# Depthwise-convolution taps on TensorE: full-array diagonal matmuls, or 16 tiles of 32x32 with four taps at a time

## The reference, cut to what matters

```python
D_MODEL, SEQ, CONV_WIDTH = 1024, 512, 31

def causal_dwconv(x, w, b):             # x: (B, S, C), w: (31, C)
    y = lax.conv_general_dilated(x, w[:, None, :], window_strides=(1,), padding=[(30, 0)],
        dimension_numbers=("NWC", "WIO", "NWC"), feature_group_count=c)
    return y + b

def conformer_conv_module(h, w_in, b_in, dw, dw_b, ln_g, ln_b, w_out, b_out):
    u = h @ w_in + b_in                                  # 1024 -> 2048
    u = u[..., :D_MODEL] * jax.nn.sigmoid(u[..., D_MODEL:])
    u = causal_dwconv(u, dw, dw_b)                       # 31 taps, each channel alone
    u = layer_norm(u, ln_g, ln_b)
    u = jax.nn.silu(u)
    return u @ w_out + b_out
```

## Time and profile before

| | us |
|---|---|
| median of 3 runs | 3459.36 (3456.99 to 3459.85) |
| the profiled execution, device time | 3458.37 |
| its span, first to last instruction | 3456.6 |
| PE busy | 3280.9 (95%) |
| DVE busy | 1811.6 (52%) |
| ACT busy | 1227.3 (36%) |
| POOL busy | 138.6 (4%) |

### The profile page before, as it was taken

How to read it: one execution, slowest core, us unless ns; L and a number is a source line. 1 busy time by engine, 2 the same in 40 slices (tenths; PEclk the granted TensorE clock), 3 DMA queues, 4 the chain that set the end, 5 groups by cost and what they waited for, 6 DMA issues and landing times.

```text
span 3456.6 us, 41804 instructions
## 1 busy us (share of the span) xinstructions
PE 3280.9 (95%) x16765; PEld 2676.6 (77%) x16765; DVE 1811.6 (52%) x2360; ACT 1227.3 (36%) x1664; POOL 138.6 (4%) x148
## 2 busy tenths in 40 slices
PE   7889999999998899999999988999999999999999
PEld 6666888888876478888888647888788888888887
DVE  3756445554446744455536965554434524456543
ACT  2525224343334432344424324443312212244432
POOL 1121000000021300000000010000000000000000
PEclk9999999999999899999999989999999999999999
DMA  5220322222341122222232112222221221223222
GB/s 153 54 71 25 98 97 97 87 96 97 98 105 47 37 63 96 97 98 97 91 104 74 49 55 86 97 91 91 92 93 61 74 74 62 86 68 105 94 92 85
DMA packets 231695, 288.16 MB, mean 83 GB/s; under 512 B 5396, under 2 KB 188716, under 8 KB 231564
## 3 DMA queue, kind: packets, MB, share of 16 engines
q1 hardware_dynamic: 225628, 266.89, 23.7%
q0 software_dynamic: 5936, 19.40, 2.6%
HBM read 284.18 MB, written 2.10 MB: 83 GB/s over the span
## 4 chain that ended last, share of the span: by engine, by line
PE 88%; DVE 7%; ACT 3%; issue 2%; DMA 0%; DVEq 0%; POOL 0%; ACTq 0%; POOLq 0%
PE ps L1398 18%; PE ps L1399 18%; PE ps L1400 18%; PE ps L1495 6%; PE ps L1496 6%; PE ps L1497 6%; PE ps L1431 2%; PE ps L1433 2%; PE ps L1432 2%; PE ps L1564 2%; PE ps L1600 2%; PE ps L1744 1%; ACT t_whi L577 1%; DVE t_wlo L905 1%; PE ps L1838 1%
## 5 line engine op out<-in xcount | busy, mean ns | idle before, releaser
L905 DVE TENSOR_TENSOR t_wlo<-t_wraw,t_whi 128x2048 fp32r<-128x2048 f32 x252 | 578.7, 2296 | 1324.6 <-ACT t_whi L577 1324.6
L1398 PE MATMUL ps<-t_hh,t_whi 128*128 128x512 f32 (+1 forms) x2624 | 985.4, 376 | 45.4 <-DVE t_hl L975 27.1
L577 ACT ACTIVATE t_whi<-t_wraw 128x2048 fp32r<-128x2048 f32 x252 | 482.7, 1916 | 1472.7 <-PE ps L1400 981.8
L1399 PE MATMUL ps<-t_hl,t_whi 128*128 128x512 f32 (+1 forms) x2624 | 977.8, 373 | 0.0
L1400 PE MATMUL ps<-t_hh,t_wlo 128*128 128x512 f32 (+1 forms) x2624 | 977.6, 373 | 0.0
L1398 PEld LDWEIGHTS ps<-t_hh,t_whi 128*128 128x128 f32 x2624 | 502.8, 192 | 136.9 <-issue 22.5
L1399 PEld LDWEIGHTS ps<-t_hl,t_whi 128*128 128x128 f32 x2624 | 502.6, 192 | 85.1 <-issue 2.0
L1400 PEld LDWEIGHTS ps<-t_hh,t_wlo 128*128 128x128 f32 x2624 | 502.4, 191 | 83.9
L1497 PE MATMUL ps<-t_whi,t_midl 128*128 128x512 f32 x704 | 273.9, 389 | 0.0
L1495 PE MATMUL ps<-t_whi,t_midh 128*128 128x512 f32 x704 | 273.9, 389 | 0.0
L1496 PE MATMUL ps<-t_wlo,t_midh 128*128 128x512 f32 x704 | 273.9, 389 | 0.0
(11 more groups left out here) (246 smaller groups left out, 3968.0 us busy)
## 6 DMA issues: line engine op xcount, KB each, us to landing
t_wraw<-in_w_in_dram SPq DMA_DIRECT2D x46, 1024.0 KB, 5.3
t_wraw<-in_w_up_dram SPq DMA_DIRECT2D x44, 1024.0 KB, 5.1
t_wraw<-in_ffn_w_in_dram SPq DMA_DIRECT2D x44, 1024.0 KB, 5.0
t_wraw<-in_w_kv_dram SPq DMA_DIRECT2D x24, 1024.0 KB, 5.2
t_wraw<-in_w_down_dram SPq DMA_DIRECT2D x20, 1024.0 KB, 5.0
t_wraw<-in_ffn_w_out_dram SPq DMA_DIRECT2D x20, 1024.0 KB, 5.0
t_wraw<-in_w_branch_dram SPq DMA_DIRECT2D x12, 1024.0 KB, 5.0
t_wraw<-in_w_q_dram SPq DMA_DIRECT2D x12, 1024.0 KB, 5.1
```

What stands on the lines that cost most here:

```text
L577: sc.activation(whi[slot][:, :], wraw[slot][:, :], ACT.Copy).then_inc(w_hi, 1)
L905: v.tensor_tensor(wlo[slot][:, :], wraw[slot][:, :], whi[slot][:, :].bitcast(F32), ALU.subtract).then_inc(w_lo, 1)
L1398: te.matmul(out, wh, xh, start=first, stop=False)
L1399: te.matmul(out, wh, xl, start=False, stop=False)
```

## The change

The taps on TensorE no longer use the whole array for one tap. A weight is now a diagonal of 32x32 for 32 channels, and the array is used as 16 tiles: four groups of 32 channels (rows of the array, index i) times four taps (columns, index g). `partial_taps(t)` (L1799 of the changed kernel) issues, for each four taps of a channel tile, 16 matmuls of 32x32 by 512; tap g of channel group i goes to PSUM bank `part_bank(t, i)`, partitions 32g to 32g + 31. So each channel has four partial sums, on four groups of partitions. ACT copies the four banks to SBUF (`copy_partials`, L889), and `join_taps(t)` (L1807) adds the four partial sums with one matmul for each channel group, whose weight is four 32x32 identities stacked (`stack`, a new constant). DVE adds the result to `vb` (`add_joined`, L1327).

With it other things change. PE takes 16 taps of each of the first six tiles and 20 of the last two (`pe_taps`), where it took 10; DVE takes 15, 15, 15 and 11 in the four steps (DVE_TAPS), where it took 21. The diagonals are made by POOL, one instruction for a channel tile (`tap_diagonals`, L565), from `stack`, which POOL loads first. The mean of the layer norm takes two matmuls: POOL adds up the tiles 0 to 6 (`usum`, L578 and L581) as they become complete, and PE multiplies `usum` and the last tile.

The order on PE is another: the taps of tile t stand between the two halves (`row_tile`) of a weight chunk, and the join behind the second half. The taps of the next tile wait until DVE has added the joined sum of this one (`tap_added`), since they share the banks 4 to 7; only the last tile has banks of its own (0 to 3). DVE adds the even tile's sum in the middle of its own taps, ahead of tap 12, and the odd tile's sum after the next step's gate.

```diff
@@ -37,7 +37,7 @@
 TAPS = 31
-PE_TAPS = 10
+DVE_TAPS = (15, 15, 15, 11)
 GRID = 64
...
@@ -204,7 +204,8 @@
             ub, vb = sb("ub", KT * UW, stack=s), sb("vb", KT * T, stack=s)
-            tapd = sb("tapd", 4 * PE_TAPS * P, stack=s)
+            tapd = [sb(f"tapd{i}", 20 * 32, stack=s) for i in range(2)]
+            part, usum, stack = sb("part", 8 * T, stack=s), sb("usum", T, stack=s), sb("stack", 32, stack=s)
         with ExitStack() as s:
...
@@ -347,6 +348,14 @@
             return (0, 2) if j == 0 else (4 * j - 2, 4 * j + 2)
+        def pe_taps(t):
+            return TAPS - DVE_TAPS[t // 2]
+        def part_bank(t, i):
+            return bank(4 + i) if t < KT - 1 else bank(i)
...
@@ -545,6 +554,32 @@
                 gains(2 * l + 1)
+            def tap_diagonals(t):
+                n = pe_taps(t)
+                if t >= 2:
+                    pool.wait_ge(tapped, t - 1)
+                r0 = ROWS["cm_dw_2"][0] + 8 * DVE_TAPS[t // 2] + t
+                w = pvec[:, r0:r0 + 8 * (n - 1) + 1:8].rearrange("p (n o) -> p n o", o=1).broadcast_to([P, n, 32])
+                eye = stack[:, :].rearrange("p (o m) -> p o m", o=1).broadcast_to([P, n, 32])
+                gp.tensor_tensor(tapd[t % 2][:, 0:32 * n].rearrange("p (n m) -> p n m", n=n), eye, w,
+                                 ALU.mult).then_inc(taps_in, 1)
+            pool.wait_ge(h_lo, SPLIT["pre4"] + 8)
+            pool.dma_start(stack[:, :], A["c_stack"]).then_inc(stack_in, 16)
+            pool.wait_ge(stack_in, 16)
+            tap_diagonals(0)
+            tap_diagonals(1)
+            for t in range(KT - 1):
+                if t + 2 < KT:
+                    tap_diagonals(t + 2)
+                pool.wait_ge(convolved, t + 1)
+                if t == 1:
+                    ins = gp.tensor_tensor(usum[:, :], tile(vb, 0), tile(vb, 1), ALU.add)
+                elif t > 1:
+                    ch.link(ins)
+                    ins = gp.tensor_tensor(usum[:, :], usum[:, :], tile(vb, t), ALU.add)
+            ins.then_inc(usum_done, 1)
             add_squares()
...
@@ -845,26 +880,28 @@
-            def tap_diagonals(j):
-                if j >= 2:
-                    act.wait_ge(tapped, 2 * (j - 1))
-                for m in range(2):
-                    t = 2 * j + m
-                    for i in range(PE_TAPS):
-                        at = ((t % 4) * PE_TAPS + i) * P
-                        ins = sc.activation(tapd[:, at:at + P], ident, ACT.Copy, scale=col("cm_dw_2", 8 * (TAPS - PE_TAPS + i) + t))
-                    ins.then_inc(taps_in, 1)
+            def copy_partials(t):
+                act.wait_ge(tapped, t + 1)
+                if t >= 2:
+                    act.wait_ge(joined, t - 1)
+                for i in range(4):
+                    sc.activation(tile(part, 4 * (t % 2) + i), part_bank(t, i), ACT.Copy).then_inc(part_out, 1)
...
             for j in range(4):
+                if j:
+                    copy_partials(2 * j - 2)
                 hi(c + 2 * j)
+                if j:
+                    copy_partials(2 * j - 1)
                 hi(c + 2 * j + 1)
...
                     sc.activation(tmp[m], cm_bank(j, 1, m), ACT.Sigmoid, bias=col("cm_b_in_2", 8 + 2 * j + m)).then_inc(u_sig, 1)
-                tap_diagonals(j)
+            copy_partials(KT - 2)
+            copy_partials(KT - 1)
             for t in range(KT):
...
@@ -1282,11 +1319,16 @@
-            def add_tapped(j):
-                for m in range(2):
-                    ch.wait(last[m])
-                    dve.wait_ge(tapped, 2 * j + m + 1)
-                    v.tensor_tensor(tile(vb, 2 * j + m), tile(vb, 2 * j + m), bank(4 + m), ALU.add).then_inc(convolved, 1)
+            def add_joined(t, done=None):
+                m = t % 2
+                ch.wait(last[m])
+                dve.wait_ge(joined, t + 1)
+                ins = v.tensor_tensor(tile(vb, t), tile(vb, t), part_bank(t, 0), ALU.add)
+                ins.then_inc(tap_added, 1)
+                dve.wait_ge(tap_added, t + 1)
+                if done:
+                    v.memset(small[:, 16:17], 0.0).then_inc(convolved, 1)
...
@@ -1307,10 +1349,12 @@
                 if j:
-                    add_tapped(j - 1)
+                    add_joined(2 * j - 1, True)
                 dve.wait_ge(u_ready, 2 * j + 2)
                 last = [0, 0]
-                for k in range(TAPS - PE_TAPS):
+                for k in range(DVE_TAPS[j]):
+                    if k == 12:
+                        add_joined(2 * j)
                     for m in range(2):
...
@@ -1321,7 +1365,11 @@
                                                                  in1=tile(vb, t), op0=ALU.mult, op1=ALU.add))
-            add_tapped(3)
+                if j < 3:
+                    ch.wait(last[0])
+                    v.memset(small[:, 16:17], 0.0).then_inc(convolved, 1)
+            add_joined(KT - 2, True)
+            add_joined(KT - 1, True)
             dve.wait_ge(summed, 1)
...
@@ -1408,14 +1456,19 @@
+            def row_tile(c, bufs, m, o):
+                s = c % 2
+                for k in range(KT):
+                    wh, wl = (w[s][:, k * CW + m * P:k * CW + (m + 1) * P] for w in (whi, wlo))
+                    ins = mm3(o, wh, wl, tile(bufs[0], k), tile(bufs[1], k), k == 0, k == KT - 1)
+                return ins
             def rows_out(c, bufs, bank0=None, tiles=2):
-                s = c % 2
-                b0 = 2 * s if bank0 is None else bank0
+                b0 = 2 * (c % 2) if bank0 is None else bank0
                 for m in range(tiles):
-                    for k in range(KT):
-                        wh, wl = (w[s][:, k * CW + m * P:k * CW + (m + 1) * P] for w in (whi, wlo))
-                        ins = mm3(bank(b0 + m), wh, wl, tile(bufs[0], k), tile(bufs[1], k), k == 0, k == KT - 1)
+                    ins = row_tile(c, bufs, m, bank(b0 + m))
                 return ins
...
@@ -1731,41 +1784,47 @@
             c, d = FIRST["cm_in"], DRAINS["cm_in"]
-            def taps(j):
-                for m in range(2):
-                    t = 2 * j + m
-                    pe.wait_ge(taps_in, t + 1)
-                    pe.wait_ge(u_ready, t + 1)
-                    if j:
-                        pe.wait_ge(convolved, t - 1)
-                    for i in range(PE_TAPS):
-                        at, u0 = ((t % 4) * PE_TAPS + i) * P, t * UW + TAPS - PE_TAPS + i
-                        ins = te.matmul(bank(4 + m), tapd[:, at:at + P], ub[:, u0:u0 + T], start=i == 0, stop=i == PE_TAPS - 1)
-                    ins.then_inc(tapped, 1)
-            def ln_mean(j):
-                for t in (2 * j, 2 * j + 1):
-                    pe.wait_ge(convolved, t + 1)
-                    ins = te.matmul(bank(7), meanm, tile(vb, t), start=t == 0, stop=t == KT - 1)
-                if j == 3:
-                    ins.then_inc(summed, 1)
+            def partial_taps(t):
+                pe.wait_ge(taps_in, t + 1)
+                pe.wait_ge(u_ready, 2 * (t // 2) + 2)
+                if t and t < KT - 1:
+                    pe.wait_ge(tap_added, t)
+                n = pe_taps(t)
+                for r in range(n // 4):
+                    for i in range(4):
+                        for g in range(4):
+                            q, p = 4 * r + g, 32 * i
+                            u0 = t * UW + DVE_TAPS[t // 2] + q
+                            ins = te.matmul(part_bank(t, i)[32 * g:32 * g + 32, :], tapd[t % 2][p:p + 32, 32 * q:32 * q + 32],
+                                            ub[p:p + 32, u0:u0 + T], start=r == 0, stop=r == n // 4 - 1)
+                ins.then_inc(tapped, 1)
+            def join_taps(t):
+                pe.wait_ge(part_out, 4 * t + 4)
+                for i in range(4):
+                    ins = te.matmul(part_bank(t, 0)[32 * i:32 * i + 32, :], stack[:, :], tile(part, 4 * (t % 2) + i), start=True, stop=True)
+                ins.then_inc(joined, 1)
...
                     first_two(c, "pre4")
-                else:
-                    for i in range(2):
-                        start(c + 2 * j + i, d=d + 2 * j + i)
-                        rows_out(c + 2 * j + i, (hh, hl), bank0=2 * (1 - i)).then_inc(w_used, 1)
-                if j:
-                    taps(j - 1)
-                if j > 1:
-                    ln_mean(j - 2)
-            taps(3)
-            ln_mean(2)
-            ln_mean(3)
+                    continue
+                for i in range(2):
+                    start(c + 2 * j + i, d=d + 2 * j + i)
+                    row_tile(c + 2 * j + i, (hh, hl), 0, cm_bank(j, i, 0))
+                    partial_taps(2 * (j - 1) + i)
+                    row_tile(c + 2 * j + i, (hh, hl), 1, cm_bank(j, i, 1)).then_inc(w_used, 1)
+                    join_taps(2 * (j - 1) + i)
+            partial_taps(KT - 2)
+            partial_taps(KT - 1)
+            join_taps(KT - 2)
+            join_taps(KT - 1)
+            pe.wait_ge(usum_done, 1)
```

(7 more changed lines are left out.)

## The result

| | before | after |
|---|---|---|
| median of the runs, us | 3458.52 (4 runs) | 3434.28 (3431.99 to 3440.68, 4 runs) |
| profiled execution, us | 3458.37 | 3431.99 |
| its span, us | 3456.6 | 3430.1 |
| stage: first L975 / L1012 of DVE to first L1327 / L1375, us | 164.70 | 140.34 |

The ratio is 0.9933, with a 95% interval of 0.9916 to 0.995: 24 us faster. Forecast were 26.5 us less in the profiled execution, and 3432 us. (The four runs of before are the three of the first table and one more.) The two stages differ by 24.36 us; the stage of the changed kernel starts 1.0 us earlier in its span, and the last 1.1 us of the 26.5 between the spans lie behind it.

A forecast was written before the change was run, and what follows sets the result against it. PE, busy 95% of 3456.6 us, sets the first three steps and DVE the last; the walk's end moves from 2026.9 to 2000.4, gaining 26.5 us: 3458.4 - 26.5 = 3432 us, range 3423 to 3455.

The forecast's parts named there:

- P: PE's time for a tile's 64 small matmuls: 3.5 to 4.4 us estimated, 4.4 taken.
- J: PE's join of a tile's partial sums, one round of four column groups: 1.06 us.
- half a chunk between small matmuls: PE's half weight chunk, between whose neighbours the taps and join stand: 5.45 us.
- DVE's loss beside POOL: DVE's taps slowed by POOL's sum and diagonals: 0 to 2.9 us a step, 1.5 taken.
- period: From one odd chunk's end to the next, the longer path, through DVE: 33.9 us.
- PE's own period: PE's path between ends of odd chunks, 21.8 + 2P + 2J: 32.7 us.
- the 7.0 of the first: Issue-bound rival: PE cannot start small matmuls faster, P 7.0 to 8.3 us, time say 3455; chance 0.13.
- the 7.9 that 0.062 us for each record would make: Within the issue-bound rival: 62 ns decoding for each of 128 records, P 7.9 us, time 3458.
- the 13.9 of the second: Four-abreast rival: only one array division works at once, P 13.9 us, time 3509; chance 0.15 for four or fewer.
- E3: End of chunk 3 on PE, 1900.4 + 2P + J: 1910.3 us.
- just covered: PE's last two tiles' taps, 2.5 P = 11 us; PE's path ends at 1999.2, beside 2000.4.
- the tail: The mean and what follows the last sum: unchanged, within 1.5 us either way.

The follow-up runs named there:

- e5: Changed kernel with DVE adding the even tile's joined sum ahead of tap 10, not 12, in steps 0 to 2: 3431.73 us, ratio 0.9925.
- e7: Changed kernel with even sum ahead of tap 10, ACT's sigmoid ahead of `hi`, DVE's second `lo` behind gate and odd sum (step 3: all additions): 3429.47 us.
- e9: e7 with a fourth move: POOL sums only tiles 0 to 5, and PE multiplies that sum, then tiles 6 and 7: 3430.41 us, ratio 0.9917.
- e3: Changed kernel with every round of 16 small matmuls issued twice, same result: 3469.81 us, one run.
- e10: e9 with the taps of each of the first six tiles in two pieces, mid-half-chunk and at its end: 3429.62 us.
- e8: The changed kernel itself, unaltered, measured again: 3435.18 us, ratio 0.9931.
- e4: Changed kernel with small matmuls reordered, all rounds of one 32-channel group before the next group: 3496.95 us, one run.

## Why the prediction was right, and where it was lucky

| step | forecast | measured |
|---|---|---|
| P, 64 small matmuls | 4.4 | 4.40 |
| J | 1.06 | 0.99 |
| half a chunk between small matmuls | 5.45 | 5.67 |
| four copies on ACT | 2.16 | 2.07 |
| DVE's loss beside POOL, a step | 1.5 | 1.8, 2.0 |
| period | 33.9 | 34.43, 34.66 |
| PE's own period | 32.7 | 33.5 (in e5, e7, e9) |
| PE's wait ahead of odd tiles' taps | 1 to 2 | 0.91, 1.13 |
| `lo` of the odd chunk waiting for ACT | 4 | 5.14, 4.69, 4.68 |
| first L1375, on before's clock | 2004 | 2005.8 |

**P was the number that decided**, and its source held. L1633 in the earlier trace rows took 1.06 us for two matmuls; a round of sixteen takes 1.06 too (e3). Record by record the sixteen first passes of a tile's first round start within 0.1 us and the second ones come 0.45 us later; further on, records start some 0.017 us apart: no issue bound. The rivals fall with that: P lies far from the 7.0 of the first, from the 7.9 that 0.062 us for each record would make, and from the 13.9 of the second. The 64 matmuls are 64 x 0.86 = 55 us of whole-array time in 4.40, 12.5 times as fast; the 10.6 times that the Trainium skill gives (TensorE: Matmul & The Clock Gate, Measured speedup vs the span model) would have made 5.2, and the measurement decides for the row.

**What is late next** was named rightly: the mid-step addition of DVE. Its wait shows in the chain, and e5 takes it away.

**Three terms were too small.** The half chunks: 0.22 us each for the change of shape; the prediction had put that cost wholly within P and J. E3 came 0.9 later by it (1911.2 on before's clock for 1910.3). POOL's loss: 0.3 to 0.5 a step more, with half a chunk's 0.2 the whole of the 0.5 and 0.8 in the periods. And the step that has the last taps: its first taps lose 0.97 beside POOL, which the prediction had put at nothing there. Together the last sum of POOL ended 3.3 us late, at 2003.7 on before's clock for 2000.4: 0.9 from E3, 1.3 from the periods, 1.0 from these first taps.

PE was forecast at 11 us for the last two tiles, "just covered"; it took 12.80, having waited 5.30 us and started at the lower clock. The last addition waited 0.34 us for it, which cost nothing: the chain goes through the addition before and POOL's sum.

```profile
1985.00:1993.00 8.00, 7.46 (x174) 4.35 (x182) 7.96 (x13) 0.00 (x0) 1.50 (x1) 0.69 0.36 130
1993.00:1998.00 5.00, 5.00 (x162) 3.78 (x149) 5.00 (x9) 2.06 (x4) 0.00 (x0) 1.00 0.02 3
```

(columns as in the earlier trace rows; the clock was 0.69 in the first stretch and 1.00 in the second). In e9, where PE had waited only 1.88 us, the clock was 1.00 throughout, and the same taps took 10.80 us. The wait alone does not settle it: in e10, behind the same 1.88, the clock was 0.50 from 1987 to 1989 us, and they took 12.39.

**One term was too large**, the tail, forecast as unchanged. Before, the two matmuls of the mean took 3.80 us, behind 8.26 us of idle PE:

```profile
2026.33 3.78 PE L1751 MATMUL ps<-t_vb,t_base 128*128 128x512 f32 x4 [8.26 <-DVE t_vb L1289]
```

After, they took 1.13 and 0.87, behind 1.2 idle. The granted clock was 0.50 from 2026.3 to 2030.2 us before, and 1.00 from 2002.7 to 2004.8 after. From the last thing that the mean waits for (DVE's last addition before, POOL's last sum after) to the first subtraction it is 2.1 us in place of 3.3.

So the stage gained 24.4 us and not 26.5: 3.3 less by the terms above, and 1.2 given back by the tail, which lies within its 1.5 either way. That the two errors partly cancel is luck too. That the profiled executions differ by 26.4 is chance: 2.1 of the spans' 26.5 us come from outside the stage, and only 1.1 in the second profile of the same kernel (e8). The medians, 24.2 and 24.0 us apart in two sets of runs, agree with the stage.

## What to carry over

To price a matmul that uses a small part of the array, look in the trace for matmuls that already share it: here the round of sixteen cost the 1.06 us that the pair cost. Issue such matmuls so that neighbours in the queue go to different tiles (the order by row groups doubled their time), and in few and long runs, since each place where they stand among others cost 0.2 us here, and a further break in a tile's taps 0.37. Once the bottleneck engine is relieved, look at each wait of the step anew: four moves of waits were worth 6.0 us of the stage here, a quarter of what the change itself gained in it.

## What was not expected of the hardware

- One POOL instruction of 1.05 us alone took 11.85 us beside DVE's multiply-adds (row above), and ended 1.03 us behind the start of DVE's addition from PSUM; the 22 multiply-adds took 14.66 us, so DVE lost nothing in them. In step 1 the same line took 1.27 and DVE lost 0.8. In the versions with three and four moves one such instruction took 9.0 to 9.2 us in each of steps 0 to 2. The Trainium skill (SBUF — State Buffer, SBUF: two separate sides) says that POOL and certain operations of DVE, those with two inputs in SBUF among them, exclude each other, and that the one that starts first keeps the other waiting for its whole length. The first tap's 1.51 us, which begin 0.29 behind the start of POOL's addition and end 0.28 behind its end, fit that, if the tap is one of these operations; a wait over some sixteen of DVE's instructions goes beyond it. What decides which of the two waits is left open.
- The mean's f32 matmul over 512 columns took 1.13 us after 1.2 us of idle PE, at a granted clock of 1.00, and 2.07 after 1.7 (e5), at 0.50: where the clock falls in a short gap, a short stretch behind it takes nearly twice as long.
- Small matmuls that run four abreast after a gap stayed at a granted clock of 0.50 for all of 44.78 us (e4), although PE was busy throughout, while sixteen abreast, after the same gap, showed 0.69 from 1985 to 1993 us and then 1.00.
